# Router to first expert product in fewer steps: masks, ranks and first hits shortened, residual products ahead of them, gather and turn in halves

## The chip, the cores and the metric

The kernel runs on one core of one Trainium2 chip. The metric is the device time of one execution in microseconds (us), as the median over several executions.

## What is computed

Two layers (DEPTH = 2) over 256 tokens of width 1024, all in float32. Each layer adds to the residual stream x first a mixer (three kinds of heads, not touched here), then a mixture of experts. The latter, cut to what matters:

```python
gl = (xf @ w_group) + b_group                 # 4 groups; xf = rmsnorm(x, norm2_g)
pg = softmax(gl); g_sel = argmax(gl)
el = (xf @ w_expert) + b_expert               # 4 groups x 8 experts
top_v, top_i = lax.top_k(el[g_sel], 2)        # the best two of the group's eight
wts = softmax(top_v) * pg[g_sel]
eid = g_sel * 8 + top_i
# each of the 32 experts, on the tokens sent to it:
h = silu(xb @ w_gate[e]) * (xb @ w_up[e])     # 1024 -> 512
out = sum over the token's two experts of wts * (h @ w_down[e])
x = x + out
```

Each expert has three matrices of 2 MB, so a layer reads 96 of them.

## The kernel before

The tokens lie in two tiles of 128 partitions (NT = 2, index j), xres holds the residual stream token by token. Each engine has its own instruction list, written out by hand in the order in which it runs; semaphores (s_...) order them against each other. `V.drain()` on VectorE waits until the engine's earlier operations have landed, so that the next may read them.

**Expert stage.** Experts go in 16 pairs (NPAIR). One pass handles up to 32 tokens (UT) of each expert of a pair: 64 slots. A pair takes as many passes as its fuller expert needs, which is known on the chip only; the counts go to `ctl`, and the engines read their loop bounds from there. A pass (`one_pass` on each engine) does the gate product (L1462, kind 0, from `xTe`), adds the last pass's result to the sums in PSUM banks 4 to 7 (`combine`, L1434), does the up product (L1462, kind 1), gathers the rows of the next pass (`gather`, L1415: `hit` times xres), turns hx and the weighted hits (L1475, L1479), turns the gathered rows (L1424, weights `rows_g[r, k::KD]`) and does the down product (L1499). ScalarE copies the gathered rows from PSUM (L602), VectorE builds the next hits (L851, L854), the SwiGLU (L874 to L881) and `xTe` (L843, a multiply by the norm's gain).

**The ring.** Weights pass through ten tiles of 2 MB, loaded by SyncE's queue in the order of use. A tile's next load waits for the product that used it (`tile_free`). The first ten matrices of a layer are loaded during the mixer as its buffers come free; the last two of them wait for the mixer's output product.

**Router to first expert product**, the stretch that the change rewrites. TensorE turns xres (L1402), runs one product that nobody reads (`busy(1)`, L1810), then the router product (L1818, 36 columns: 4 groups, 32 experts) into bank 0. Four more such products follow, then TensorE waits for the masks (s_mk). VectorE reads the logits (L1279), takes maxima and their indices for the group and then for the experts of the group (L1286 to L1304), and makes the masks `mk` and their sum `mks` (L1314, L1316). TensorE then computes for each token how many earlier ones went to each expert, and each expert's count, all in bank 1 (L1825 to L1829), puts xres into banks 4 to 7 by a product with the identity (L1832), and waits for the hits of the first pair (s_hit0). VectorE makes these from the ranks of experts 0 and 1 (L1330 to L1337, then L851, L854), then the slot of every token, the number of passes per pair and the control values (L1340 to L1379, s_ctl), reads two of these back into registers (L1381, L1382) and only then waits for the turned rows and makes `xTe` (s_xte0). SyncE and GpSimd wait for s_ctl too, before they load the next layer's small parameters. ScalarE computes two exponentials of the router (L805, L807) between.

## Time and profile before

| | |
|---|---|
| median of 3 executions | 1297.69 us (1297.36 to 1298.72) |
| the profiled execution | 1291.37 us |
| its span, from the first instruction to the last | 1289.6 us |
| TensorE busy | 1070.8 us (83%) |
| VectorE, ScalarE, GpSimd busy | 460.6, 179.9, 23.7 us |
| DMA | 440.56 MB, mean 342 GB/s |
| chain that ended last | PE 52%, DMA 41%, DVE 3%, issue 2% |

The tables of the profile are read so. PE is TensorE, PEld its weight loads, DVE VectorE, ACT ScalarE, POOL GpSimd, SPq the queue of SyncE. A line like L1462 is a line of the kernel. A float32 product shows as two matmul records. "issue" is time in which an engine waited for nothing that the profile shows, its own register work among it; DVEq is the engine's sequencer. The granted clock (PEclk) is the share of TensorE's full clock of 2.4 GHz, so 0.50 is 1.2 GHz. Durations of one engine's operations overlap a little, so the chain's pieces, not the durations, add up.

### The profile page before, as it was taken

The page shows a single profiled execution, that of the slowest core. Times are in us where ns is not written, and L with a number is a line of the kernel's source. Part 1 is how long each engine was busy: PE and PEld are TensorE (multiplying, and loading weights), DVE is VectorE, ACT ScalarE, POOL GpSimd, SP SyncE. Part 2 cuts the span into 40 slices and gives each one's busy share as a digit, 9 for nine tenths or more (in the row PEclk, how much of TensorE's full clock was granted, in tenths as well). Part 3 has the DMA queues.
Part 4 walks back from the last instruction along what each step waited for, and adds up shares of the span by engine and source line. Part 5 has one row for each costly group of instructions (what it writes and reads, how often), then busy time and mean ns, then how long its engine had stood idle before and what let it go on. Part 6 is the DMA issues. An engine that isn't in the chain of part 4 may idle for free.

```text
span 1289.6 us, 23165 instructions
## 1 busy us (share of the span) xinstructions
PE 1070.8 (83%) x9476; PEld 576.8 (45%) x9477; DVE 460.6 (36%) x1253; ACT 179.9 (14%) x427; POOL 23.7 (2%) x36
## 2 busy tenths in 40 slices
PE   5999999997887766776799999898767777679966
PEld 3476654453333333333355755543333333334433
DVE  0786445433232222222237753533222222224321
ACT  2224310010010000000024160100000000001000
POOL 3000002000000000000000000000000000000000
PEclk8999999998998888888899999998888888889988
DMA  9621378999999999999993313799999999996997
GB/s 313 228 104 66 137 296 288 383 427 426 426 427 427 426 427 426 426 427 427 387 332 140 131 66 131 326 376 427 426 424 427 428 426 428 425 426 277 428 428 297
DMA packets 50270, 440.56 MB, mean 342 GB/s; under 512 B 9313, under 2 KB 11521, under 8 KB 25089
## 3 DMA queue, kind: packets, MB, share of 16 engines
q1 hardware_dynamic: 48112, 435.79, 81.7%
q0 software_dynamic: 960, 1.51, 0.7%
q10 hardware_dynamic: 1104, 1.85, 0.5%
q8 instruction: 79, 1.29, 0.4%
q14 instruction: 15, 0.11, 0.0%
HBM read 437.56 MB, written 1.05 MB: 340 GB/s over the span
## 4 chain that ended last, share of the span: by engine, by line
PE 52%; DMA 41%; DVE 3%; issue 2%; DVEq 1%; ACT 0%; SPq 0%; ACTq 0%
DMA ring<-in_e_w_up_dram 24%; PE PS L1462 12%; DMA ring<-in_e_w_down_dram 9%; PE PS L1525 8%; DMA ring<-in_e_w_gate_dram 7%; PE PS L1499 6%; PE PS L1761 4%; PE PS L1519 3%; PE PS L1424 3%; PE PS L1415 3%; PE PS L1434 2%; DMA gT<-in_norm_g_dram 1%; PE PS L1695 1%; PE PS L1715 1%; PE PS L1475 1%
## 5 line engine op out<-in xcount | busy, mean ns | idle before, releaser
L1462 PE MATMUL PS<-ring,hT 128*32 128x256 f32 x4608 | 336.5, 452 | 171.6 <-DMA ring<-in_e_w_gate_dram 112.4
L1462 PEld LDWEIGHTS PS<-ring,hT 128*32 128x32 f32 x4608 | 182.6, 125 | 347.0 <-issue 283.4
L1499 PE MATMUL PS<-ring,hT 128*32 128x512 f32 x1152 | 137.1, 618 | 11.5 <-DMA ring<-in_e_w_down_dram 11.5
L874 DVE TENSOR_SCALAR hT<-hT 128x256 f32<-128x256 f32 x36 | 10.6, 294 | 334.1 <-ACT hT L607 334.1
L1525 PE MATMUL PS<-ring,hT 128*128 128x512 f32 x256 | 113.1, 595 | 0.0
L1424 PE MATMUL PS<-cst,mixT 64*64 64x64 f32 x1216 | 81.2, 282 | 5.8 <-ACT mixT L602 1.4
L1424 PEld LDWEIGHTS PS<-cst,mixT 64*64 64x64 f32 x1216 | 77.1, 212 | 15.0 <-issue 11.8
L1415 PE MATMUL PS<-xres,scr 128*64 128x512 f32 x304 | 73.6, 605 | 0.0
L1499 PEld LDWEIGHTS PS<-ring,hT 128*32 128x32 f32 x1152 | 36.4, 113 | 82.7 <-issue 80.8
L1434 PE MATMUL PS<-hT 64*128 64x512 f32 x288 | 71.8, 615 | 0.0
L1525 PEld LDWEIGHTS PS<-ring,hT 128*128 128x128 f32 x256 | 47.5, 190 | 53.6 <-issue 53.6
L881 DVE TENSOR_TENSOR hT<-hT,PS 128x256 f32<-128x256 f32 x36 | 15.2, 421 | 156.5 <-PE PS L1462 156.5
L602 ACT COPY mixT<-PS 128x512 f32<-128x512 f32 x38 | 22.2, 585 | 335.7 <-PE PS L1415 335.7
L876 DVE RECIPROCAL hT<-hT 128x256 f32<-128x256 f32 x36 | 63.1, 1753 | 2.6
L1761 PE MATMUL PS<-ring,mixT 128*128 128x512 f32 x128 | 57.8, 599 | 2.1 <-DVE mixT L1262 1.9
L607 ACT ACTIVATE hT<-PS 128x256 f32<-128x256 f32 x36 | 13.8, 383 | 292.8 <-PE PS L1462 292.8
L612 ACT COPY hT<-PS 128x512 f32<-128x512 f32 x36 | 21.1, 585 | 221.4 <-PE PS L1499 221.4
L843 DVE TENSOR_TENSOR hT<-PS,gT 128x512 f32<-128x512 f32 x38 | 26.3, 692 | 70.2 <-PE PS L1424 70.2
L1519 PE MATMUL PS<-hT,ring 128*128 128x256 f32 x192 | 45.6, 399 | 2.6 <-ACT hT L625 2.6
L1519 PEld LDWEIGHTS PS<-hT,ring 128*128 128x128 f32 x192 | 38.2, 201 | 9.1 <-issue 3.7
L883 DVE COPY hT<-PS 128x256 f32<-128x256 f32 x36 | 15.3, 425 | 74.8 <-PE PS L1479 74.8
L1434 PEld LDWEIGHTS PS<-hT 64*128 64x128 f32 x288 | 25.5, 186 | 32.1 <-issue 32.1
(342 smaller groups left out, 898.4 us busy)
## 6 DMA issues: line engine op xcount, KB each, us to landing
ring<-in_e_w_gate_dram SPq DMA_DIRECT2D x64, 2048.0 KB, 38.6
ring<-in_e_w_up_dram SPq DMA_DIRECT2D x64, 2048.0 KB, 39.8
ring<-in_e_w_down_dram SPq DMA_DIRECT2D x60, 2048.0 KB, 37.3
ring<-in_w_in_dram SPq DMA_DIRECT2D x10, 2048.0 KB, 18.5
ring<-in_w_out_dram SPq DMA_DIRECT2D x2, 4096.0 KB, 13.0
ring<-in_e_w_down_dram SPq DMA_DIRECT2D x8, 1024.0 KB, 38.7
ring<-in_w_in_dram SPq DMA_DIRECT2D x2, 1024.0 KB, 23.2
xres<-in_x_dram ACTq DMA_DIRECT2D x1, 1024.0 KB, 9.9
```

The source lines that it names most:

```text
L602: act.copy(rows_g, PS[:, 0, :]).then_inc(gs, 1)
L612: act.copy(Y, PS[:, 3, :]).then_inc(s_ys, 1)
L843: V.tensor_tensor(xTe, PS[:, 0, :].rearrange("p (k s) -> p k s", k=KD), bcast(gT[:, l, 1, :], PAIR), ALU.mult).then_inc(xte, 1)
L876: V.reciprocal(es, es)
L1415: last = pe.matmul(PS[64 * h:64 * h + 64, 0, :], hit[:, j, :], xres[:, j, 512 * h:512 * h + 512], start=j == 0, stop=j == NT - 1)
L1424: last = pe.matmul(PS[r, 0, PAIR * k:PAIR * k + PAIR], rows_g[r, k::KD], ident[r, r], start=True, stop=True)
L1434: pe.matmul(PS[:, 4 + 2 * j + h, :], hitT[r, j, :], Y[r, :], start=False, stop=False)
L1462: last = pe.matmul(PS[o:o + UT, bank, 0:256], xTe[:, k, UT * u:UT * u + UT], w[u][:, k, :, 2 * h:2 * h + 2], start=k == 0, stop=k == KD - 1)
L1499: last = pe.matmul(PS[o:o + UT, 3, :], hTe[:, c % 2, hc:hc + UT], w[u][:, c, 512 * h:512 * h + 512], start=c == 0, stop=c == KF - 1)
L1519: last = pe.matmul(PS[:, bank, T * half:T * half + T], wchunk(c)[:, k, col:col + P], hT[:, k, :], start=k == 0, stop=k == KD - 1)
L1525: last = pe.matmul(PS[:, bank, :], hT[:, k, P * j:P * j + P], wchunk(c)[:, k, 0:512], start=k == 0, stop=k == KD - 1)
L1761: last = pe.matmul(PS[:, OUT_BANK[n], :], mixT[:, k, P * j:P * j + P], wout[:, k, 512 * h:512 * h + 512], start=k == 2, stop=k == 1)
```

## The change

All of it lies between the router product and the middle of the first expert product of each layer.

- TensorE: the product without a reader ahead of the router product goes, and the four behind it. In their place, ahead of the wait for the masks, come the products that put xres into banks 4 to 7. The ranks of both token tiles come from two products over 64 columns (`mks` has a block of zeros ahead for that) and raise s_rk by themselves; the counts come from two products into bank 2 with a semaphore of their own (s_cn); then one product without a reader, and the wait for the hits.
- VectorE: the group logits go straight into `gl8`, the expert logits into `lg`; memsets move ahead. The sum and reciprocal of the group exponentials, and the weights `wgt`, move behind the first pair's rows. The first hits come from one operation over the ranks and the summed masks, and four compares of 32 columns straight into `hit`. Then passes per pair and control values (s_ctl), then `xTe` in two halves, then the slots of all tokens and the weights, and then the two register reads.
- The first gather is done in halves of 256 columns into banks 0 and 3, with the columns of xres read in the order k, p (a step of 8 words), so that `rows_g` holds each k contiguously. ScalarE copies each half, TensorE turns each half, VectorE multiplies each half; s_gath0, s_gs0, s_rT0 and s_xte0 count twice per layer. The first expert product waits for the first half at its start, and for the second ahead of k = 4.

```diff
@@ -805,7 +803,9 @@
                 act.activation(pex, pex, ACT.Exp).then_inc(s_rge, 1)
                 act.wait_ge(s_rv, l + 1)
                 act.activation(dif, dif, ACT.Exp).then_inc(s_rve, 1)
-                rows_gathered(s_gath0, s_gs0, l)
+                for c in range(2):
+                    act.wait_ge(s_gath0, 2 * l + c + 1)
+                    act.copy(rows_g[:, 256 * c:256 * c + 256], PS[:, (0, 3)[c], 0:256]).then_inc(s_gs0, 1)
                 wait_apart(act, s_ctl, l + 1)
                 total = act.value_load(c_tot, min_val=NPAIR, max_val=MAXN - 1)
                 p0 = act.value_load(c_p0, min_val=0, max_val=(L - 1) * (MAXN - 1))
...
@@ -1272,30 +1269,33 @@
                 norm_rows(l, 1)
 
 
+                V.memset(gl8, -3.0e38)
+                V.memset(mks[:, 0, :], 0.0)
+                V.drain()
                 parameters(dve, 2, l)
                 dve.wait_ge(s_rp, l + 1)
                 dve.wait_ge(s_rs, 2 * l + 2)
                 for j in range(NT):
-                    V.scalar_tensor_tensor(lg[:, j, :], PS[:, 0, 64 * j:64 * j + 36], rs[:, j:j + 1], rb[:, :], ALU.mult,
-                                           ALU.add)
-                V.memset(gl8, -3.0e38)
-                V.drain()
-                V.tensor_copy(gl8[:, :, 0:4], lg[:, :, 0:4])
+                    V.scalar_tensor_tensor(gl8[:, j, 0:4], PS[:, 0, 64 * j:64 * j + 4], rs[:, j:j + 1], rb[:, 0:4],
+                                           ALU.mult, ALU.add)
+                for j in range(NT):
+                    V.scalar_tensor_tensor(lg[:, j, :], PS[:, 0, 64 * j + 4:64 * j + 36], rs[:, j:j + 1], rb[:, 4:36],
+                                           ALU.mult, ALU.add)
                 V.drain()
                 for j in range(NT):
                     V.max(gmx[:, j, :], gl8[:, j, :])
                 V.drain()
                 for j in range(NT):
                     V.max_index(idx[:, 0, j, :], gmx[:, j, :], gl8[:, j, :])
-                V.tensor_tensor(pex, lg[:, :, 0:4], gmx[:, :, 0:1].broadcast_to([P, NT, 4]), ALU.subtract).then_inc(s_rg, 1)
                 V.drain()
                 V.tensor_copy(gsel, idx[:, 0, :, 0:1])
                 V.drain()
 
                 gid = cst[:, C_GID:C_GID + NE].unsqueeze(1).broadcast_to([P, NT, NE])
                 V.tensor_tensor(elp, gid, gsel.broadcast_to([P, NT, NE]), ALU.not_equal)
-                V.drain()
-                V.scalar_tensor_tensor(elp, elp, NEG, lg[:, :, 4:36], ALU.mult, ALU.add)
+                V.tensor_tensor(pex, gl8[:, :, 0:4], gmx[:, :, 0:1].broadcast_to([P, NT, 4]), ALU.subtract).then_inc(s_rg, 1)
+                V.drain()
+                V.scalar_tensor_tensor(elp, elp, NEG, lg, ALU.mult, ALU.add)
                 V.drain()
                 for j in range(NT):
                     V.max(emx[:, j, :], elp[:, j, :])
@@ -1305,82 +1305,83 @@
                 V.tensor_tensor(dif, emx[:, :, 1:2], emx[:, :, 0:1], ALU.subtract).then_inc(s_rv, 1)
                 V.drain()
                 V.tensor_copy(eid, idx[:, 1, :, 0:2])
-                dve.wait_ge(s_rge, l + 1)
-                V.tensor_reduce(pgs, pex, X, ALU.add)
-                V.drain()
-                V.reciprocal(pgs, pgs)
+                V.drain()
                 iota_e = cst[:, C_T:C_T + NE].unsqueeze(1).broadcast_to([P, NT, NE])
                 for a in range(2):
                     V.tensor_tensor(mk[:, a], iota_e, eid[:, :, a:a + 1].broadcast_to([P, NT, NE]), ALU.is_equal)
                 V.drain()
-                V.tensor_tensor(mks, mk[:, 0], mk[:, 1], ALU.add).then_inc(s_mk, 1)
+                V.tensor_tensor(mks[:, 1:], mk[:, 0], mk[:, 1], ALU.add).then_inc(s_mk, 1)
+                V.memset(Y, 0.0)
+                V.memset(hitT, 0.0)
+                V.drain()
+
+
+                ranks = PS[:, 1, 0:64].rearrange("p (j n) -> p j n", j=NT)
+                dve.wait_ge(s_rk, l + 1)
+                V.scalar_tensor_tensor(fsh, ranks[:, :, 0:2], 1.0, mks[:, 1:, 0:2], ALU.add, ALU.mult)
+                V.drain()
+                for j in range(NT):
+                    for u in range(2):
+                        last = V.tensor_scalar(hit[:, j, UT * u:UT * u + UT], cst[:, C_T + 1:C_T + 1 + UT], fsh[:, j, u:u + 1],
+                                               rs[:, j:j + 1], ALU.is_equal, ALU.mult)
+                last.then_inc(s_hit0, 1)
+
+
+                dve.wait_ge(s_cn, l + 1)
+                nf = nu.rearrange("p i u -> p (i u)")
+                V.tensor_scalar(nf, PS[:, 2, 0:NE], 1.0, 1.0 / UT, ALU.max, ALU.mult)
+                V.tensor_copy(rnk, ranks)
+                V.drain()
+                V.tensor_scalar(nf, nf, 31.0 / 64, ROUND, ALU.add, ALU.add)
+                V.tensor_scalar(fr32, rnk, 1.0 / UT, -31.0 / 64, ALU.mult, ALU.add)
+                V.drain()
+                V.tensor_scalar(nf, nf, -ROUND, None, ALU.add)
+                V.drain()
+                V.tensor_tensor(npass, nu[:, :, 0], nu[:, :, 1], ALU.max)
+                V.drain()
+                V.tensor_tensor_scan(pend, cst[:, C_ONES:C_ONES + NPAIR], npass, 0.0, ALU.mult, ALU.add)
+                V.tensor_copy(ctl[:, C_NP:C_NP + NPAIR], npass[0:1, :])
+                V.tensor_copy(c_p0, past[:, 0:1])
+                V.drain()
+                V.tensor_scalar(upr, pend[0:1, :], past[:, 0:1], None, ALU.add)
+                V.tensor_copy(c_tot, pend[0:1, NPAIR - 1:NPAIR])
+                V.drain()
+                V.tensor_copy(ctl[:, C_PASS + 1:C_PASS + 1 + NPAIR], upr).then_inc(s_ctl, 1)
+                V.tensor_copy(past[:, 0:1], upr[:, NPAIR - 1:NPAIR])
+                for c in range(2):
+                    dve.wait_ge(s_rT0, 2 * l + c + 1)
+                    V.tensor_tensor(xTe[:, 4 * c:4 * c + 4, :], PS[:, (0, 3)[c], 0:256].rearrange("p (k s) -> p k s", k=4),
+                                    bcast(gT[:, l, 1, 4 * c:4 * c + 4], PAIR), ALU.mult).then_inc(s_xte0, 1)
+
+                V.tensor_scalar(fr32, fr32, ROUND, -ROUND, ALU.add, ALU.add)
+                V.tensor_tensor(pst[:, :, 0], pend, npass, ALU.subtract)
+                V.drain()
+                V.scalar_tensor_tensor(rnk, fr32, float(UT), rnk, ALU.mult, ALU.add)
+                V.tensor_scalar(pst[:, :, 1], pst[:, :, 0], float(PAIR), float(UT), ALU.mult, ALU.add)
+                V.tensor_scalar(pst[:, :, 0], pst[:, :, 0], float(PAIR), None, ALU.mult)
+                V.drain()
+                V.tensor_tensor(rnk, rnk, rv[:, 160:192].unsqueeze(1).broadcast_to([P, NT, NE]), ALU.add)
+                dve.wait_ge(s_rge, l + 1)
+                V.tensor_reduce(pgs, pex, X, ALU.add)
+                V.drain()
+                for a in range(2):
+                    V.tensor_tensor(rtm[:, a], mk[:, a], rnk, ALU.mult)
+                V.reciprocal(pgs, pgs)
                 dve.wait_ge(s_rve, l + 1)
                 V.tensor_scalar(wgt[:, :, 0:1], dif, 1.0, None, ALU.add)
                 V.drain()
+                V.tensor_reduce(sh.rearrange("p a j -> p (a j)"), rtm.rearrange("p a j n -> p (a j) n"), X, ALU.add)
                 V.reciprocal(wgt[:, :, 0:1], wgt[:, :, 0:1])
                 V.drain()
+                V.tensor_copy(sw, sh)
                 V.tensor_tensor(wgt[:, :, 0:1], wgt[:, :, 0:1], pgs, ALU.mult)
                 V.drain()
+                V.tensor_scalar(sh, sh, -float(PAIR), None, ALU.add)
                 V.tensor_tensor(wgt[:, :, 1:2], wgt[:, :, 0:1], dif, ALU.mult)
-                V.memset(Y, 0.0)
-                V.memset(hitT, 0.0)
-
-                dve.wait_ge(s_rk, l + 1)
-                ranks = PS[:, 1, 0:64].rearrange("p (j n) -> p j n", j=NT)[:, :, 0:2]
-                V.tensor_tensor(fpl, ranks, cst[:, C_T + 1:C_TT:UT].unsqueeze(1).broadcast_to([P, NT, 2]), ALU.add)
-                for a in range(2):
-                    V.scalar_tensor_tensor(fmk[:, a], ranks, UT - 0.5, mk[:, a, :, 0:2], ALU.is_lt, ALU.mult)
-                V.drain()
-                for a in range(2):
-                    V.tensor_tensor(fmk[:, a], fmk[:, a], fpl, ALU.mult)
-                V.drain()
-                V.tensor_reduce(fsh.rearrange("p a j -> p (a j)"), fmk.rearrange("p a j u -> p (a j) u"), X, ALU.add)
-                V.drain()
-                row_hits(s_hit0, cst[:, C_T + 1:C_TT], fsh)
-                V.tensor_copy(rnk, PS[:, 1, 0:64].rearrange("p (j n) -> p j n", j=NT))
-                V.tensor_copy(cnt, PS[:, 1, 64:96])
-                V.drain()
-                nf = nu.rearrange("p i u -> p (i u)")
-                V.tensor_scalar(nf, cnt, 1.0, 1.0 / UT, ALU.max, ALU.mult)
-                V.tensor_scalar(fr32, rnk, 1.0 / UT, -31.0 / 64, ALU.mult, ALU.add)
-                V.drain()
-                V.tensor_scalar(nf, nf, 31.0 / 64, ROUND, ALU.add, ALU.add)
-                V.drain()
-                V.tensor_scalar(nf, nf, -ROUND, None, ALU.add)
-                V.drain()
-                V.tensor_tensor(npass, nu[:, :, 0], nu[:, :, 1], ALU.max)
-                V.tensor_scalar(fr32, fr32, ROUND, -ROUND, ALU.add, ALU.add)
-                V.drain()
-                V.tensor_tensor_scan(pend, cst[:, C_ONES:C_ONES + NPAIR], npass, 0.0, ALU.mult, ALU.add)
-                V.scalar_tensor_tensor(rnk, fr32, float(UT), rnk, ALU.mult, ALU.add)
-                V.drain()
-                V.tensor_tensor(pst[:, :, 0], pend, npass, ALU.subtract)
-                V.drain()
-                V.tensor_scalar(pst[:, :, 1], pst[:, :, 0], float(PAIR), float(UT), ALU.mult, ALU.add)
-                V.tensor_scalar(pst[:, :, 0], pst[:, :, 0], float(PAIR), None, ALU.mult)
-                V.drain()
-                V.tensor_tensor(rnk, rnk, rv[:, 160:192].unsqueeze(1).broadcast_to([P, NT, NE]), ALU.add)
-                V.drain()
-                for a in range(2):
-                    V.tensor_tensor(rtm[:, a], mk[:, a], rnk, ALU.mult)
-                V.drain()
-                V.tensor_reduce(sh.rearrange("p a j -> p (a j)"), rtm.rearrange("p a j n -> p (a j) n"), X, ALU.add)
-                V.drain()
-                V.tensor_copy(sw, sh)
-                V.drain()
-                V.tensor_scalar(sh, sh, -float(PAIR), None, ALU.add)
-
-                V.tensor_scalar(upr, pend[0:1, :], past[:, 0:1], None, ALU.add)
-                V.tensor_copy(c_p0, past[:, 0:1])
-                V.tensor_copy(c_tot, pend[0:1, NPAIR - 1:NPAIR])
-                V.tensor_copy(ctl[:, C_NP:C_NP + NPAIR], npass[0:1, :])
-                V.drain()
-                V.tensor_copy(past[:, 0:1], upr[:, NPAIR - 1:NPAIR])
-                V.tensor_copy(ctl[:, C_PASS + 1:C_PASS + 1 + NPAIR], upr).then_inc(s_ctl, 1)
+                V.drain()
                 wait_apart(dve, s_ctl, l + 1)
                 total = dve.value_load(c_tot, min_val=NPAIR, max_val=MAXN - 1)
                 p0 = dve.value_load(c_p0, min_val=0, max_val=(L - 1) * (MAXN - 1))
-                rows_turned(l, s_rT0, s_xte0, l)
                 with dve.Fori(0, total) as q:
                     one_pass(l, p0 + q)
@@ -1456,6 +1457,8 @@
 
                     w = [t.rearrange("p (k n c) -> p k n c", k=KD, c=KF) for t in weights(kind)]
                     for k in range(KD):
+                        if kind == 0 and k == KD // 2:
+                            pe.wait_ge(s_xte0, 2 * l + 2)
                         for h in range(2):
                             for u in range(2):
                                 o = 64 * h + UT * u
@@ -1463,7 +1466,7 @@
                                                  w[u][:, k, :, 2 * h:2 * h + 2], start=k == 0, stop=k == KD - 1)
                     last.then_inc(s_used[kind], 1)
 
-                pe.wait_ge(s_xte0, l + 1)
+                pe.wait_ge(s_xte0, 2 * l + 1)
                 pe.wait_ge(s_xte, n + 1)
                 in_product(0, 1)
                 combine(n)
@@ -1807,10 +1810,9 @@
                 def busy(n):
 
                     for k in range(n):
-                        pe.matmul(PS[:, 4 + 2 * (k % 2), :], ident, cst[:, 0:512], start=True, stop=True)
+                        pe.matmul(PS[:, 3, :], ident, cst[:, 0:512], start=True, stop=True)
 
                 turn_xs(l, 1)
-                busy(1)
                 parameters(pe, 2, l)
                 for j in range(NT):
                     turned_xs(l, 1, j)
@@ -1819,21 +1821,34 @@
                                          start=k == 0, stop=k == KD - 1)
                 last.then_inc(s_rp, 1)
 
-                busy(4)
-                pe.wait_ge(s_mk, l + 1)
-                bef = cst[:, C_BEFORE:C_BEFORE + P]
-                pe.matmul(PS[:, 1, 0:NE], bef, mks[:, 0, :], start=True, stop=True)
-                pe.matmul(PS[:, 1, NE:2 * NE], ones, mks[:, 0, :], start=True, stop=False)
-                pe.matmul(PS[:, 1, NE:2 * NE], bef, mks[:, 1, :], start=False, stop=True)
-                pe.matmul(PS[:, 1, 2 * NE:3 * NE], ones, mks[:, 0, :], start=True, stop=False)
-                pe.matmul(PS[:, 1, 2 * NE:3 * NE], ones, mks[:, 1, :], start=False, stop=True).then_inc(s_rk, 1)
                 for j in range(NT):
                     for h in range(2):
                         pe.matmul(PS[:, 4 + 2 * j + h, :], ident, xres[:, j, 512 * h:512 * h + 512], start=True, stop=False)
+                pe.wait_ge(s_mk, l + 1)
+                flat_mks = mks.rearrange("p j n -> p (j n)")
+                bef = cst[:, C_BEFORE:C_BEFORE + P]
+                pe.matmul(PS[:, 1, 0:2 * NE], bef, flat_mks[:, NE:3 * NE], start=True, stop=False)
+                pe.matmul(PS[:, 1, 0:2 * NE], ones, flat_mks[:, 0:2 * NE], start=False, stop=True).then_inc(s_rk, 1)
+                pe.matmul(PS[:, 2, 0:NE], ones, mks[:, 1, :], start=True, stop=False)
+                pe.matmul(PS[:, 2, 0:NE], ones, mks[:, 2, :], start=False, stop=True).then_inc(s_cn, 1)
+                busy(1)
+
                 pe.wait_ge(s_hit0, l + 1)
-                gather(s_gath0)
-                pe.wait_ge(s_gs0, l + 1)
-                turn_gathered(s_rT0)
+                for c in range(2):
+                    for j in range(NT):
+                        for h in range(2):
+                            half = xres[:, j, 512 * h:512 * h + 512].rearrange("t (p k) -> t k p", k=KD)
+                            last = pe.matmul(PS[64 * h:64 * h + 64, (0, 3)[c], 0:256], hit[:, j, :], half[:, 4 * c:4 * c + 4, :],
+                                             start=j == 0, stop=j == NT - 1)
+                    last.then_inc(s_gath0, 1)
+                for c in range(2):
+                    pe.wait_ge(s_gs0, 2 * l + c + 1)
+                    for k in range(4 * c, 4 * c + 4):
+                        for h in range(2):
+                            r = slice(64 * h, 64 * h + 64)
+                            last = pe.matmul(PS[r, (0, 3)[c], PAIR * (k % 4):PAIR * (k % 4) + PAIR],
+                                             rows_g[r, 64 * k:64 * k + 64], ident[r, r], start=True, stop=True)
+                    last.then_inc(s_rT0, 1)
 
                 wait_apart(pe, s_ctl, l + 1)
 
```

## Rows read from the trace of the kernel before

**Rows 1.** Windows: us, busy per engine (instructions), granted clock, DMA share, GB/s

```profile
198.60:200.60 2.00, 1.93 (x9) 0.47 (x8) 1.63 (x12) 0.03 (x1) 0.00 (x0) 1.00 0.67 287
...
831.00:833.20 2.20, 2.14 (x32) 2.00 (x32) 1.09 (x9) 0.00 (x0) 0.00 (x0) 1.00 0.38 160
...
834.80:838.20 3.40, 3.40 (x33) 1.93 (x37) 2.26 (x11) 0.00 (x0) 0.00 (x0) 0.50 0.00 0
...
193.40:198.60 5.20, 5.20 (x12) 2.14 (x11) 4.29 (x27) 0.00 (x0) 0.00 (x0) 0.70 1.02 438
...
240.00:250.00 10.00, 10.00 (x144) 4.95 (x138) 3.04 (x6) 0.97 (x2) 0.00 (x0) 1.00 0.72 277
...
380.00:640.00 260.00, 181.94 (x1846) 90.69 (x1840) 57.42 (x160) 15.59 (x34) 0.00 (x0) 0.86 1.01 426
```

**Rows 2.** Chain of waits, layer 0: start us, us, what

```profile
180.95 1.94 PE PS L1402 x16
182.89 0.86 PE PS L1810 x2
183.75 3.51 PE PS L1818 x32
...
191.87 0.24 DVE so L1316
...
192.15 0.41 PE PS L1825 x2
...
193.23 0.42 PE PS L1829 x2
193.66 5.00 PE PS L1832 x8
198.66 1.89 PE PS L1415 x8
...
200.57 0.59 ACT mixT L602
...
201.21 2.16 PE PS L1424 x32
...
204.55 3.83 PE PS L1462 x64
```

**Rows 3.** Timeline, both layers: start us, us, engine, line, operation, tiles

```profile
181.88 2.25 ACT L625 ACTIVATE hT<-PS,gT 128x128 f32<-128x128 f32 x8 [2.45 <-PE PS L1402]
...
208.66 0.93 SPq L507 DMA_DIRECT2D ring<-in_e_w_down_dram  x2
...
824.79 3.68 PE L1832 MATMUL PS<-xres,cst 128*128 128x512 f32 x8
...
834.79 5.43 PE L1462 MATMUL PS<-ring,hT 128*32 128x256 f32 x64 [1.63 <-DVE hT L843]
```

**Rows 4.** Chain of waits, layer 1

```profile
815.58 3.51 PE PS L1818 x32
...
823.37 0.23 DVE so L1316
...
832.36 0.32 DVEq L1381
...
833.64 0.70 DVE hT L843
```

**Rows 5.** Groups by line and shape, 187 to 206: count, busy us, mean ns, idle before

```profile
L851 DVE TENSOR_SCALAR scr<-cst,so,small 128x64 f32<-128x64 f32 x5 | 1.3, 312 | 0.1
...
L1325 DVE MEMSET hT<- 128x512 f32 x1 | 0.5, 485 | 0.1
...
L1344 DVE TENSOR_SCALAR vm<-vm 128x32 f32<-128x32 f32 x1 | 0.2, 181 | 0.1
```

**Rows 6.** The page's groups over both layers

```profile
L876 DVE RECIPROCAL hT<-hT 128x256 f32<-128x256 f32 x36 | 63.1, 1753 | 2.6
L607 ACT ACTIVATE hT<-PS 128x256 f32<-128x256 f32 x36 | 13.8, 383 | 292.8 <-PE PS L1462 292.8
```

26 lines of the change are left out of this document (11 added, 15 removed).

## Prediction

> **What bounds the kernel now.** I read the windows first. From 250 us to the last product of layer 0 the DMA engines are full: the row 380:640 has DMA share 1.01 at 426 GB/s while PE works 182 of 260 us. The expert stage is a stream of 2 MB matrices, and nothing that shortens PE inside it counts. What does count is when the stream is released. The ten ring tiles are filled ahead; the fill ends in row 198.6:200.6 (share 0.67 of 2.0 us, so at 199.9) and in row 831:833.2 (0.38 of 2.2, so at 831.8), and row 834.8:838.2 has the DMA at nothing [rows 1]. It waits for the first expert product to give tiles back: SP issues the next pair of matrices at 208.66, right behind that product (204.55 to 208.38) [rows 2, 3]. So the start of the first product sets the start of the stream, in each of the two layers. The stretch before 250, with the DMA at 277 GB/s in 240:250 [rows 1], hangs on PE, which started with the same product. A microsecond taken out between the mixer and the first product should arrive at the end of the kernel as a microsecond, twice.
>
> Then I read the chain of waits through that stretch. Layer 0 [rows 2]: router product until 187.26 (183.75 + 3.51), masks ready at 192.11 (191.87 + 0.24), rank and count products until 193.66, the residual products until 198.66, gather 1.89, copy 0.59, turn until 203.37, first product at 204.55. So 17.29 us from the router product's end. The chain goes over PE: the hits wait finished while PE works off the residual products. These took 5.00 us at a granted clock of 0.70 in that stretch (1.2 GHz part of the time) [rows 1]; in layer 1 the same took 3.68 [rows 3]. Layer 1 [rows 4]: router product until 819.09, masks at 823.60 (823.37 + 0.23), first product at 834.79, 15.70 us. There the chain goes through DVE, whose list of rank and control steps and two value loads (832.36 to 833.64) holds back the last multiply; and the first product itself took 5.43 us at clock 0.50 [rows 1, 3], against 3.83 in layer 0 [rows 2].
>
> **The change, step by step, per layer.**
> (a) Router product. The cover product ahead of it goes (0.86 in the chain [rows 2]). What is next to be late is ACT's half of hT: 8 operations from 181.88 in 2.25 us [rows 3], so the first four end at about 183.0 (estimate, half the time); a weight load behind that gives a start at about 183.3 instead of 183.75. I take 0.4 of a possible 0.86.
> (b) Router product to masks. Before, 4.51 us in layer 1 and 4.85 in layer 0 [rows 2, 4]; layer 0's surplus has no operation to it. A copy and a memset leave the path ahead of the first maximum, two more operations from PSUM enter: I take 0.1 gained. The sum and the reciprocal of the group's exponentials leave the stretch between the expert index and the masks; one dependent step is about 0.26 (0.18 for a small operation [rows 5] and 0.08 of drain): 0.2 gained. So 4.2 in layer 1; in layer 0, 4.5.
> (c) Masks to gather. PE: residual products already done: 3.68 us from the router product's end, against 4.2 to 4.5 for the masks, so they are off the path by 0.5 us (at the low clock, 5.0, they would be late by that much). Then 4 small products instead of 5: of the 5 the first took 0.41, the middle three 0.22 each ((193.23 - 192.15 - 0.41)/3), the last 0.42 [rows 2]. Four are 0.05 + 0.41 + 2x0.22 + 0.42 = 1.3; ranks alone, two of them, are ready at 0.9. Then one cover product, 0.92 (a quarter of 3.68 [rows 3]): PE is free for the gather 2.3 after the masks. DVE: the two memsets (0.49 and about half of that for the smaller one [rows 5]) plus drain are done at 0.8, so DVE waits for the ranks until 0.9; one operation and drain 0.25; four of 128x32. Of 128x64 four take 4x0.31 at most; at 32 wide a similar one is 0.18 [rows 5]: 0.7. Hits at 1.85. The new wait is for PE's cover product, not for the hits: gather at 2.3. Before it was 6.55 in layer 0 and 4.9 in layer 1 (824.79 + 3.68) [rows 2, 3].
> (d) Gather. Same columns in two halves: 1.9 [rows 2]. The moving operand now steps 8 words (32 bytes). No row has that as moving operand. Nearest below: the turn of xres reads its stationary operand with that step, 16 in 1.94 = 0.121 us each, against 0.110 (3.51/32) for contiguous ones in the router product [rows 2], at most 10% more. Nearest in the number of streams: the expert product reads four streams with two words in every 16 bytes at 3.83 for 64 [rows 2], which is as many different 16-byte stretches per time as two streams of single words. I take no price; bounds 0 and 1.9.
> (e) Copies and turns. The copy of half 0 (0.38 for 128x256, 0.59 for 128x512 [rows 2, 6]) runs under the gather of half 1, that of half 1 under the turn of half 0 (half of 2.16). So gather and turn stand back to back: 1.9 + 2.15. The turn now reads contiguous rows; I take nothing for it (at most 0.2).
> (f) Turn to first product. Only half 0 of xTe is needed: its multiply (0.70 at 512 wide [rows 4], so some 0.4) runs under the turn of half 1. What is left is PE's own register work (two value loads, tile waits). Before, product minus end of turn was 1.18 in layer 0 with 0.70 of DVE in it: between 0.45 and 1.18 remains, since the cover of that multiply is gone. I take 0.8, nearer the middle. The product's wait for half 1 at its middle comes 1.9 us in, when that multiply is long done.
> (g) SP and GpSimd wait for the control values, which come about 4 us after the masks (1.85 to the hits and some eight dependent steps of 0.26), where in layer 1 they now come 8.8 after them (832.36 [rows 4]). In layer 0 their small parameter loads then start under the end of the ring's fill. The last two matrices of the fill are for the second pair, which PE reaches more than 11 us after the first product's start (rival 2); cost nothing, and 6 us of delay would still be hidden.
>
> Sum from masks: 2.3 + 1.9 + 2.15 + 0.8 = 7.15. Layer 0: 187.26 - 0.4 + 4.5 + 7.15 = 198.5 against 204.55: 6.0. Layer 1: 819.09 - 0.4 + 4.2 + 7.15 = 830.0 against 834.79: 4.8. Together 10.8. Clock: layer 1 gets back 5.43 - 3.83 = 1.6 if its first product runs at full clock; the stretches of idle PE are shorter than before (1.2 and 1.6 ahead of the product), but not gone. I reckon with one low spell left among the two layers, -1.5. Net **10.9 us**.
>
> The page's execution took 1291.37 us with a span of 1289.6: by the sum 1280.5 and 1278.7. The median shown is 1297.69, 6.3 above the profiled execution; I lay the same difference on it: **1286.8 us**. The cap: the stream can't be released before the ring's fill ends. It ends at 199.9 and 831.8, release is now expected at 198.5 + 3.9 = 202.4 and 830.0 + 3.9 = 833.9. Two microseconds remain in each layer, so the gain passes, though at most 2 more per layer would.
>
> **Rivals.**
> 1. The strided gather streams at half rate. For it: two streams, each word in its own 16 bytes, and no row with it. Against it: the rows in (d). Price 1.9 per layer: 1286.8 + 3.8 = 1290.6. Beside it: the Trainium skill (Advanced Engine Details and Errata, SBUF Cachelines) says that at least two hits on a 16-byte line are needed to absorb the access latency and that a different line per access costs. It gives no figure; by that rule rival 1 or rival 4 would hold, and the stationary read at 0.121 against 0.110 bears it out only by a tenth [rows 2].
> 2. DVE is late in the first pass. What was taken off the path (slot numbers, weights: some 10 dependent steps of 0.26 to 0.45, then 1.28 for value loads [rows 4]) runs after the second multiply, to about 10.9 after the masks; two rounds of hits follow (3 us, from 0.31 an operation [rows 5]), to 13.9, which is 6.8 after the product's start; then the SwiGLU steps, about 3.4 with the reciprocal's 1.75 in them [rows 6], end at 10.2. PE asks for them at 3.8 + 1.9 + 3.8 + 1.9 = 11.4. Slack 1.2. If the list is 2.5 us longer than I count, 1.3 per layer are lost: 1289.4.
> 3. The gain is absorbed: the stream's end is set by something else than the first product (fill and parameters in one queue, the cap above). Then 1297.7. Against it: the DMA idle from 199.9 to 208.66 and at 834.8 [rows 1, 3].
> 4. Slower: the strided read costs much more than twice. One mechanism, the moving operand of the gather, 1.9 us a layer at rate 1. The gain of 10.9 is eaten at 1 + 10.9/3.8 = 3.9 times the time; at 5 times it is 1297.69 - 10.9 + 15.2 = 1302.0. Against it: stationary reads with this step.
>
> **How the numbers follow.** Forecast 0.69 (its own range 1283 to 1289.5: (a) and (f) at their good ends and no low spell give 3 to 4 less; two low spells and (f) at 1.18 give 2.3 more), rival 1 0.12, rival 2 0.06, rival 3 0.08, rival 4 0.05. Faster by over 0.2% (about what a measurement of this kernel can tell from no change, here 2.6 us) is the first three: 0.87; same 0.08; slower 0.05. The range takes the forecast's own and rival 1: 1283 to 1291.5.
>
> **What would show it.** In the profile after: residual products right behind the router product and done before the first rank product; masks about 4.2 behind the router product; gather of both halves 1.9 (3.8: rival 1; 9: rival 4); the first expert product 11.3 to 11.7 behind the router product's end, at 198.5 and, less what layer 0 gave, 11.3 behind in layer 1; the DMA idle ahead of it down from 8 to some 2 us; the stretch from first product to the layer's end as long as before (rival 3: longer by the gain; rival 2: an idle PE ahead of the transpose of hx in the first pass). Wrong would be: the first product late for registers or for code by several us, or more low-clock spells than one.

## The result and the profile after

The changed kernel takes 1290.45 us (median of 13 executions, 1286.10 to 1295.13) against 1297.36 us (13 executions, 1294.04 to 1301.60) of the kernel before: ratio 0.9946, 95% interval 0.9930 to 0.9963. So 6.9 us were gained, where 10.9 had been forecast; the forecast of 1286.8 us was 3.7 too low. The result lies inside the stated range of 1283 to 1291.5, but outside the forecast's own part of it (1283 to 1289.5), in the part that rival 1 had added. The profiled execution took 1290.15 us, with a span of 1288.3.

The chain of waits of the changed kernel in layer 0 (start us, us, what), the counterpart of [rows 2]:

```profile
182.82 0.90 PE PS L1403 x8
...
183.75 1.15 ACT hT L623 x4
...
185.03 3.73 PE PS L1820 x32
188.77 5.21 PE PS L1826 x8
193.97 0.17 PE PS L1830 x2
...
194.79 0.94 PE PS L1813 x2
195.73 3.81 PE PS L1841 x16
199.53 1.18 PE PS L1849 x32
...
200.74 0.44 DVE hT L1353
201.17 1.40 issue
202.58 5.34 PE PS L1465 x61
207.92 1.92 PE PS L1435 x8
```

L1820 is the router product, L1826 the residual products (xres into banks 4 to 7), L1830 the first rank product, L1813 the cover product (one that nobody reads), L1841 the gather, L1849 the turn, L1465 the expert product, L1435 the combine behind it. The whole stretch now runs over TensorE, but for ScalarE's four activations and one multiply of VectorE (L1353); VectorE's long list of dependent steps, which held the chain of layer 1 before [rows 4], is gone from it. Layer 1 repeats it:

```profile
814.24 0.90 PE PS L1403 x8
...
820.19 5.21 PE PS L1826 x8
825.39 0.17 PE PS L1830 x2
...
827.14 3.81 PE PS L1841 x16
830.95 1.18 PE PS L1849 x32
...
832.59 1.18 issue
833.78 5.42 PE PS L1465 x60
839.19 1.92 PE PS L1435 x8
```

**A clock for the stretch.** The mixer ahead runs identical code, yet ends at different times. So I count from the end of the mixer's last product, which is where the turn of xres starts in the chain (180.95 and 812.78 before, 182.82 and 814.24 after), and give two numbers per layer: "to start", until the first expert product starts, and "to end", until it ends (the start of the combine), since the ring's tiles are given back there. Before: 23.60 and 27.43 in layer 0, 22.01 and 27.44 in layer 1. After: 19.76 and 25.10, 19.54 and 24.95. To the start 3.8 and 2.5 were gained, to the end 2.3 and 2.5. Behind that, nothing changed in this pair of executions: from the first product's end to the start of the layer's last combine it is 439.5 us before (208.38 to 647.91) and 439.3 after (207.92 to 647.19), and in layer 1 442.8 (840.22 to 1283.03) and 442.6 (839.19 to 1281.80).

In windows of the changed kernel (columns as in [rows 1]) the clock is low in two places of this stretch, in both layers, the residual products and the first expert product; the kernel before had one such place in each layer of its first profiled execution:

```profile
188.70:194.00 5.30, 5.30 (x12) 2.29 (x11) 4.20 (x27) 0.41 (x2) 0.00 (x0) 0.68 1.00 419
...
202.60:206.00 3.40, 3.40 (x36) 1.83 (x40) 1.45 (x11) 0.00 (x0) 3.40 (x6) 0.54 0.89 127
...
820.20:825.40 5.20, 5.20 (x11) 2.18 (x10) 4.26 (x27) 0.41 (x2) 0.00 (x0) 0.68 1.02 435
...
833.80:837.20 3.40, 3.40 (x33) 1.78 (x37) 1.50 (x11) 0.00 (x0) 0.00 (x0) 0.50 0.02 7
```

### The profile page after: what moved, and what is told of

Its sections match the earlier page's. It is cut to its first block, busy times and chain, and to the rows that moved or that the text cites. A ratio compares the mean times of both kernels' runs of the same rounds, so it can differ in the third digit from the quotient of the medians.

```text
span 1288.3 us, 23141 instructions
## 1 busy us (share of the span) xinstructions
PE 1072.1 (83%) x9472; PEld 575.7 (45%) x9473; DVE 458.6 (36%) x1245; ACT 180.3 (14%) x429; POOL 23.8 (2%) x36
## 3 DMA queue, kind: packets, MB, share of 16 engines
q10 hardware_dynamic: 1104, 1.85, 0.5%
## 4 chain that ended last, share of the span: by engine, by line
PE 56%; DMA 41%; issue 1%; ACT 1%; SPq 0%; ACTq 0%; DVE 0%; DVEq 0%
DMA ring<-in_e_w_up_dram 30%; PE PS L1465 12%; PE PS L1528 9%; PE PS L1502 6%; DMA ring<-in_e_w_down_dram 6%; PE PS L1764 5%; PE PS L1425 3%; PE PS L1522 3%; DMA ring<-in_e_w_gate_dram 3%; PE PS L1416 3%; PE PS L1435 2%; PE PS L1698 1%; DMA gT<-in_norm_g_dram 1%; PE PS L1826 1%; PE PS L1718 1%
## 5 line engine op out<-in xcount | busy, mean ns | idle before, releaser
L1465 PE MATMUL PS<-ring,hT 128*32 128x256 f32 x4608 | 338.7, 454 | 172.9 <-DMA ring<-in_e_w_gate_dram 117.2
L1465 PEld LDWEIGHTS PS<-ring,hT 128*32 128x32 f32 x4608 | 182.6, 126 | 350.4 <-issue 286.8
L1502 PE MATMUL PS<-ring,hT 128*32 128x512 f32 x1152 | 134.3, 607 | 12.6 <-DMA ring<-in_e_w_down_dram 12.6
L1528 PE MATMUL PS<-ring,hT 128*128 128x512 f32 x256 | 116.5, 609 | 0.0
L1425 PE MATMUL PS<-cst,mixT 64*64 64x64 f32 x1152 | 76.9, 282 | 4.4
L1425 PEld LDWEIGHTS PS<-cst,mixT 64*64 64x64 f32 x1152 | 73.0, 212 | 11.9 <-issue 11.9
L1435 PE MATMUL PS<-hT 64*128 64x512 f32 x288 | 71.8, 615 | 0.0
L1416 PE MATMUL PS<-xres,scr 128*64 128x512 f32 x288 | 69.7, 605 | 0.0
L1764 PE MATMUL PS<-ring,mixT 128*128 128x512 f32 x128 | 60.8, 625 | 2.1 <-DVE mixT L1259 1.9
L1435 PEld LDWEIGHTS PS<-hT 64*128 64x128 f32 x288 | 25.5, 186 | 32.2 <-issue 32.2
```

Source lines behind the costliest of these rows:

```text
L1416: last = pe.matmul(PS[64 * h:64 * h + 64, 0, :], hit[:, j, :], xres[:, j, 512 * h:512 * h + 512], start=j == 0, stop=j == NT - 1)
L1425: last = pe.matmul(PS[r, 0, PAIR * k:PAIR * k + PAIR], rows_g[r, k::KD], ident[r, r], start=True, stop=True)
L1435: pe.matmul(PS[:, 4 + 2 * j + h, :], hitT[r, j, :], Y[r, :], start=False, stop=False)
L1465: last = pe.matmul(PS[o:o + UT, bank, 0:256], xTe[:, k, UT * u:UT * u + UT], w[u][:, k, :, 2 * h:2 * h + 2], start=k == 0, stop=k == KD - 1)
L1502: last = pe.matmul(PS[o:o + UT, 3, :], hTe[:, c % 2, hc:hc + UT], w[u][:, c, 512 * h:512 * h + 512], start=c == 0, stop=c == KF - 1)
L1528: last = pe.matmul(PS[:, bank, :], hT[:, k, P * j:P * j + P], wchunk(c)[:, k, 0:512], start=k == 0, stop=k == KD - 1)
```

## Experiments

All numbers of a stretch are from one profiled execution each; "to start" and "to end" are counted as above, from the mixer's last product. Ratios are to the kernel before, timed beside the run. Where no median is given, the profiled execution is the only one.

**Is it the step in the gather, or the halves?** The gather took 3.81 us where 1.9 was forecast. Two things had changed in it: the step of 8 words and the splitting. The first kernel keeps the step and gathers in one piece (ScalarE still copies in two):

```diff
...
-                for c in range(2):
-                    for j in range(NT):
-                        for h in range(2):
-                            half = xres[:, j, 512 * h:512 * h + 512].rearrange("t (p k) -> t k p", k=KD)
-                            last = pe.matmul(PS[64 * h:64 * h + 64, (0, 3)[c], 0:256], hit[:, j, :], half[:, 4 * c:4 * c + 4, :], ...)
+                for j in range(NT):
+                    for h in range(2):
+                        half = xres[:, j, 512 * h:512 * h + 512].rearrange("t (p k) -> t k p", k=KD)
+                        last = pe.matmul(PS[64 * h:64 * h + 64, 0, :], hit[:, j, :], half, start=j == 0, stop=j == NT - 1)
...
```

> Changed kernel, but the first gather is one piece again: two token tiles by two halves, 512 columns each, still read with a step of 8 words. Theory (the step costs): the gather takes 3.8 us as in two halves, because the rate of the strided read is halved. Rival (the splitting costs: shorter products, two banks): the gather takes 1.9 us as in the kernel before. Turn stays at 1.2 us, since its rows stay contiguous.

It took 1286.73 us, with a mixer that ended at 180.93. From its chain, the gather in both layers:

```profile
193.99 3.89 PE PS L1840 x8
...
198.60 1.17 PE PS L1847 x32
...
824.90 3.82 PE PS L1840 x8
```

Eight records of 512 columns, 3.89 and 3.82 us. The step halves the rate of the moving operand (1.89 without it [rows 2]), and the splitting costs nothing. The turn stays at 1.17.

**Gather, copy, turn and multiply as before, the rest of the change kept:**

```diff
...
+                rows_turned(l, s_rT0, s_xte0, l)
...
+                gather(s_gath0)
+                pe.wait_ge(s_gs0, l + 1)
+                turn_gathered(s_rT0)
...
```

> Changed kernel with gather, copy, turn and multiply as in the kernel before (contiguous read, one piece, turn with a step of 8 words); the rest of the change stays. Theory (step in the gather costs 1.9, contiguous turn gives back 1.0, register work of 1.9 us behind the last issued turn is a floor): gather 1.9, copy 0.6, turn 2.15, product 1.2 behind the turn, so 5.9 from the gather's start to the product against 6.86 and 6.64 in the changed kernel: about 0.8 us a layer faster than the changed kernel, ratio to the kernel before about 0.993. Rival (the halves pay as planned): slower than the changed kernel by 1 us or more a layer.

Median 1288.0 us, ratio 0.9928 (0.9900 to 0.9956).

```profile
195.86 1.89 PE PS L1411 x8
...
197.77 0.59 ACT mixT L600
...
198.41 2.16 PE PS L1420 x32
...
200.59 0.70 DVE hT L841
201.29 0.45 issue
201.74 3.87 PE PS L1458 x62
```

From the gather's start to the product 5.88 and 5.89 us, against 6.85 (195.73 to 202.58) and 6.64 in the changed kernel. To start 18.78 and 18.79, to end 22.66 and 22.63. So gather and turn in halves, as built, cost 1.0 and 0.75 us in the two layers instead of paying, and the whole gain comes from the other parts of the change. The timed medians go the same way, 1288.0 against 1290.45, though their intervals overlap. In this execution the first product ran at full clock besides (3.87 and 3.85 us).

**What is the wait behind the turn?** "issue" of 1.40 and 1.18 us stands behind the multiply of the second half, 1.87 and 1.65 behind the turn's end. Two products that nobody reads are put there:

```diff
                 wait_apart(pe, s_ctl, l + 1)
+                for k in range(2):
+                    pe.matmul(PS[:, 2, :], ident, cst[:, 0:512], start=True, stop=True)
```

> Changed kernel with two products without a reader (1.84 us at full clock, into bank 2) behind the turn and the wait for the control values, ahead of the value loads. Theory (behind the turn TensorE's array is idle for 1.9 us only because its sequencer loads registers): the sequencer loads them while the two products run, the first expert product starts within 0.2 us of where it did, 1.9 behind the turn, and if the idle stretch is what lets the clock fall, that product takes 3.8 us instead of 5.4, 1.5 a layer. Rival 1 (the wait is for something else, VectorE or the ring): the product starts 1.0 to 1.8 us later. Rival 2 (the clock falls for the narrow products before, not for the idle stretch): the product keeps its 5.4 us.

```profile
201.94 1.16 PE PS L1849 x32
203.10 1.91 PE PS L1855 x4
205.02 3.85 PE PS L1465 x63
```

1.91 us of products went in, and the expert product starts 1.92 behind the turn, where it started 1.87 behind it (layer 1: 1.91 against 1.65): to start 19.79 both, against 19.76 and 19.54. So the array isn't needed in this wait, and two products fit under it for nothing in layer 0 and for 0.25 us in layer 1. By itself the run doesn't tell the sequencer's own work (waits, two value loads, loop bounds, tile waits) from an event outside, which would hide the products as well; the rival's "1.0 to 1.8 us later" doesn't follow from it. The run with early value loads, further down, decides for the sequencer. The first expert product took 3.85 and 3.80 us, so it was at full clock; to end 23.64 and 23.59, 1.4 better. The timing doesn't show it: 1290.99 us, ratio 0.9958 (0.9940 to 0.9977), the same as the changed kernel within the intervals. The trace says where it went: behind the first product, to the layer's last combine, this execution needs 440.7 us (208.87 to 649.55) and 443.9 (840.21 to 1284.13), where the changed kernel has 439.3 and 442.6. That is 1.4 and 1.3 longer, all of what the full clock gave. Why the rest gets longer is not shown. And low spells lay in the mixer, which ended at 185.23, 2.4 later than in the changed kernel's first execution.

**The step where it costs nothing.** The gather is contiguous and whole; ScalarE's two copies read PSUM with the step and write k by k, and turn and multiply keep their halves (now in banks 3 and 0):

```diff
...
+                src = PS[:, 0, :].rearrange("s (p k) -> s k p", k=KD)
                 for c in range(2):
-                    act.copy(rows_g[:, 256 * c:256 * c + 256], PS[:, (0, 3)[c], 0:256]).then_inc(s_gs0, 1)
+                    act.copy(rows_g[:, 256 * c:256 * c + 256].rearrange("s (k p) -> s k p", k=4),
+                             src[:, 4 * c:4 * c + 4, :]).then_inc(s_gs0, 1)
...
```

> Changed kernel with a contiguous gather in one piece into bank 0; ScalarE's two copies read it with the step of 8 words and write k by k, turn and multiply stay in halves with contiguous rows. Theory (the step costs only where TensorE streams it): gather 1.9, first copy 0.4, turn 1.2 to 1.6 (second copy under the first half's turn), product 1.7 to 1.9 behind: 5.3 to 5.7 against 6.86 and 6.64, so 1.1 to 1.4 us a layer faster than the changed kernel. Rival (the step costs ScalarE the same way): copies of 0.8 each, turn ended 0.8 later, nothing left of the gain.

Median 1287.03 us, ratio 0.9917 (0.9890 to 0.9944).

```profile
196.03 1.89 PE PS L1418 x8
...
197.95 0.38 ACT mixT L809
...
198.37 1.17 PE PS L1845 x32
...
199.57 0.44 DVE hT L1355
200.00 1.28 issue
201.29 3.86 PE PS L1467 x60
```

The copy with the step takes 0.38 us, like one without (0.37 in the changed kernel). Gather to product 5.26 and 5.00 us; to start 18.17 and 17.91, to end 22.03 and 21.79: 3 us per layer better than the changed kernel, 1.6 of it from these parts and 1.5 from a first product at full clock. Not all of that arrives: behind the first product layer 0 needs 440.9 us here (205.15 to 646.02), 1.6 more than in the changed kernel, layer 1 the same 442.6.

**The residual products ahead of the masks**, undone: they go back behind the count products, in the place of the cover product, with `busy(4)` ahead of the wait for the masks.

```diff
-                for j in range(NT):
-                    for h in range(2):
-                        pe.matmul(PS[:, 4 + 2 * j + h, :], ident, xres[:, j, 512 * h:512 * h + 512], start=True, stop=False)
+                busy(4)
                 pe.wait_ge(s_mk, l + 1)
...
-                busy(1)
+                for j in range(NT):
+                    for h in range(2):
+                        pe.matmul(PS[:, 4 + 2 * j + h, :], ident, xres[:, j, 512 * h:512 * h + 512], start=True, stop=False)
```

> Changed kernel with the residual products back behind the rank and count products (in the place of the one cover product), and four cover products ahead of the wait for the masks, as in the kernel before. Theory of the prediction (that move takes the residual products off the path, 3.68 us less the one cover product of 0.92): the gather starts about 5.0 us behind the masks at full clock instead of 2.4, the first product 2.6 us later per layer. Rival (VectorE's hits would have come then anyway): under 1 us later.

It took 1293.22 us. Masks at 192.71, gather at 197.67: 4.96 behind them, where the changed kernel has 2.38 (193.35 to 195.73). To start 22.31 and 22.11 (182.21 to 204.52, 816.69 to 838.80) against 19.76 and 19.54: 2.56 later, as forecast. Undoing this move alone costs 2.6 us per layer, and what is left of the change then gains next to nothing: the kernel before has 22.65 and 22.0 in its later executions (below). The reverse, the move alone in the kernel before, was not run. By the trace it would gain nothing in layer 1: there the turn is done by 833.2 [rows 1], and VectorE's own list only at 833.64 [rows 4]. So the move needs the shorter list of VectorE beside it.

**The cover products.** One put back ahead of the router product:

```diff
                 turn_xs(l, 1)
+                pe.matmul(PS[:, 4, :], ident, cst[:, 0:512], start=True, stop=True)
```

> Changed kernel with the one product without a reader put back ahead of the router product. Theory (the idle and narrow stretch around the router product is what drops the clock in the residual products): these take 3.7 us instead of 5.2, the rank products start with the masks and the gather 0.3 us earlier against the masks, while the router product starts 0.3 us later; first product unchanged within 0.3. Rival (the clock falls for another reason): residual products stay at 5.2 us and all is 0.3 later.

It took 1290.98 us. The residual products stayed at 5.18 and 5.06 us: my reason for that low spell fell. To start 20.11 and 19.84, 0.3 later, as the rival has it. The first product, though, took 3.87 and 3.86. And the one ahead of the gather taken out:

```diff
-                busy(1)
```

> Changed kernel without the one cover product between the count products and the gather. Theory of the prediction (TensorE, not VectorE's hits, sets the gather's start, by the cover product): the gather starts up to 0.3 us earlier against the masks, not more, because the hits come then. Rival: the clock falls in the gather and it takes over 4.5 us instead of 3.8.

It took 1289.66 us.

```profile
194.51 0.42 DVE scr L1325 x2
194.94 0.04 issue
194.98 3.88 PE PS L1840 x15
```

Now the chain runs over VectorE's hits (L1325). The gather starts 2.27 and 2.46 behind the masks instead of 2.38 and 2.56; to start 19.70 and 19.51. The cover product cost 0.1 us. The hits come 0.1 ahead of its end, not 0.45 as step (c) has it.

**Value loads under the gather.** On the kernel with the reordering copies, the first pair is taken out of TensorE's loop, and its registers are read between gather and turn:

```diff
...
+                pe.wait_ge(s_ctl, l + 1)
+                passes0 = pe.value_load(ctl[0:1, C_NP:C_NP + 1], min_val=1, max_val=MAXN // 2)
+                past0 = pe.value_load(ctl[0:1, C_PASS:C_PASS + 1], min_val=0, max_val=L * MAXN)
                 for c in range(2):
                     pe.wait_ge(s_gs0, 2 * l + c + 1)
...
+                with pe.Fori(0, passes0) as q:
+                    one_pass(l, past0 + q, 0, 0)
+                with pe.Fori(0, 2) as i5:
+                    for i in range(1, 6):
...
```

> The kernel with the contiguous gather and the reordering copies, and the first pair taken out of TensorE's loop: its two value loads stand between the gather and the turn, where they run under the gather. Theory (1.7 to 1.9 us of register work behind the last issued turn is the floor of the first product, and most of it is the wait and the two value loads): the product starts 0.6 to 1.2 us behind the turn instead of 1.7, so 0.5 to 1.1 us a layer earlier. Rival 1 (the tile waits and the code of the pass are the floor): no gain. Rival 2 (eleven bodies of the pair in place of six cost code loading): the expert stage gets longer by several us.

Median 1285.18 us, ratio 0.9891 (0.9862 to 0.9919), the fastest of all; its interval overlaps that of the kernel it builds on.

```profile
198.57 1.89 PE PS L1418 x8
...
201.14 0.90 issue
202.04 0.70 PE PS L1848 x16
...
202.77 0.44 DVE hT L1355
203.20 0.24 issue
203.44 3.85 PE PS L1467 x64
```

The product starts 0.70 and 0.69 behind the turn instead of 1.75 and 1.49, so most of that wait was TensorE's own loads; but 0.90 and 0.68 us of them now stand ahead of the turn. Net, from the gather's start to the product 4.87 and 4.64 against 5.26 and 5.00: 0.4 us per layer. The expert stage is not several us longer for the eleven bodies of the pair: behind the first product 441.5 and 442.6 us, against 440.9 and 442.6 in the kernel that it builds on.

**Does the profiled execution of before stand for the others?** It took 1291.37 us, 6 less than the median, and by the profiled executions alone the change would have gained 1.2 us. Both kernels were profiled again, unchanged.

> The kernel before, unchanged, profiled a second time. Its first profiled execution took 1291.4 us against a median of 1297.4, and in it TensorE's clock fell on none of the mixer's products. Theory (that execution was a fast one: the low spells fall elsewhere from execution to execution, and most cost 1.5 us in the mixer or the router): here the mixer of layer 0 ends 1.5 to 4 us later than 180.95, and the stretch from there to the end of the first expert product stays at 27.4 us or above. Rival (the mixer of the changed kernel is slower than that of the kernel before): the mixer ends at 181 again.

> The same once more: theory and rival as in the run before; of interest is how far the stretch from the mixer's last product to the end of the first expert product spreads over executions of one kernel (theory: 27.4 to 30.5 us, a low spell more or less).

> The changed kernel, unchanged, profiled a second time. Theory: gather 3.8, turn 1.2 and product 1.65 to 1.9 behind the turn again in both layers; the stretch from the mixer's last product to the end of the first expert product 25.0 us, or 23.5 where no spell of the low clock meets that product.

They took 1293.29, 1295.24 and 1292.49 us. The kernel before, second time, layer 0:

```profile
204.44 0.70 DVE hT L843
205.14 0.45 issue
205.59 5.43 PE PS L1462 x64
211.02 1.92 PE PS L1434 x8
```

| | clock granted, 60 to 180 us | mixer's last product ends | to start | to end |
|---|---|---|---|---|
| before, first | 1.00 | 180.95, 812.78 | 23.60, 22.01 | 27.43, 27.44 |
| before, second | 0.97 | 182.94, 815.07 | 22.65, 22.02 | 28.08, 27.45 |
| before, third | 0.94 | 184.87, 816.98 | 22.64, 22.01 | 28.07, 27.45 |
| after, first | 0.97 | 182.82, 814.24 | 19.76, 19.54 | 25.10, 24.95 |
| after, second | 0.94 | 185.19, 813.84 | 19.71, 21.21 | 23.56, 25.07 |

The mixer of the kernel before ended 2.0 and 3.9 us later in layer 0 than in the first execution. So the changed kernel's mixer is not slower. What sets its end is how much of it met a low clock. Over all thirteen profiled executions, of either kernel and of the runs, a mean clock of 1.00 from 60 to 180 us goes with an end at 180.9 (two), 0.97 with 182.2 to 183.7 (seven), 0.94 with 184.9 to 185.7 (four). In its second and third execution the chain of the kernel before ran over VectorE in both layers; in layer 0 the low spell lay in the four cover products of L1810 (4.95 us for them) and not in the residual products, where it costs, so to start it has 22.65 in place of 23.60.

The stretch "to end" has a mean of 27.65 before and 24.67 after: 3.0 us per layer, 6.0 in the kernel, against 6.9 timed (4.8 to 9.1 by the interval). The second execution of after has a new case in layer 1: router product 4.31 and residual products 6.30 us. The rank products waited 1.9 us for the residual products, and the gather started 3.66 behind the masks in place of 2.56: the cover of step (c) can fail by 1.1 us. The run with early value loads has the same in layer 1 (4.36 and 6.25). Behind the first product that layer of the second execution took 445.2 us, where all three executions of before have 442.4 to 442.8.

## Why the prediction was right in part

The mechanism held: the stretch between mixer and first product sets the release of the stream, both layers gain, and what is gained arrives in the pair of executions compared (439.5 against 439.3 us behind it in layer 0, 442.8 against 442.6 in layer 1). Rival 3 is out, and so is rival 2: in the changed kernel the first pass runs from its up product (209.84) to its gather (213.59) to the turn (216.24) with the same distances as before (210.30, 214.06 and 216.71 there, within 0.01), with no idle TensorE. Rival 4 is out. **Rival 1 is what happened**, and other terms of the sum were off beside it. That its 1290.6 us is met within 0.2 is luck in part: the turn gave back 1.0 per layer that nobody had counted, and (b), (c) and (f) took 2.5 over both layers. Of the signs named, the idle DMA ahead of the release came out at 6 us in layer 1, not 2 (by the shares from 831.5 us on the fill ends at 833.2, and SP issues next at 839.47): the ring's fill ends 19.0 us behind the mixer, before and after, and the product came later than forecast. Step (g) held: the control values came 4.3 behind the masks (197.63), and the small parameter loads went out from 197.66 on.

- (a) Router product 0.4 earlier: from the mixer's last product to the router product's end it was 6.31, now 5.94 (182.82 to 188.76). Right in its size, by two parts that nearly cancel: the router product starts 0.6 earlier and takes 3.73 in place of 3.51. The group of four activations that it waits for is in the chain, as named.
- (b) Router product to masks 4.2 and 4.5: measured 4.40 (masks at 824.58) and 4.59 (193.35). The sum was 0.1 to 0.2 too low. In layer 1 the way to the first maximum takes 0.85 us as before (820.18 to 821.03, 819.09 to 819.94), so the four operations from PSUM eat what the copy and the memset gave, and the step taken out gave 0.1.
- (c) Masks to gather 2.3: 2.38 and 2.56. Nearly right, and the residual move is worth 2.6. But the hits were to be ready at 1.85 and came at 2.27 in the run without the cover product: the rank products ended later, and the four compares took 0.9 in place of 0.7. Not foreseen: the residual products run into the low clock, 5.21 us in place of 3.68, and end 0.6 and 0.8 behind the masks. That costs little, because the rank products then start without their first delay (0.17 for the first in the chain instead of 0.41).
- (d) **Gather 1.9: measured 3.81.** This is the step that failed. "I take no price" rested on two rows, and neither was of that kind. The stationary read with the step (0.121 against 0.110 us [rows 2]) is another operand. The four streams of the expert product have two words in every 16 bytes, and I argued that two streams of single words ask for as many 16-byte stretches. By the run with the whole gather the moving operand with one word in every 32 bytes takes twice the time. The Trainium skill's rule that was put beside rival 1 (Advanced Engine Details and Errata, SBUF Cachelines) wants at least two hits on a line. The traces agree: the factor is 2.0 for this operand and this step.
- (e) Gather and turn back to back, turn 2.15: back to back was right, but the turn took 1.18. I had allowed 0.2 for its rows being contiguous. In the stationary operand 32 records of 64 columns take 2.16 with the step and 1.17 without. By the same rule of the Trainium skill the step costs there too, and the traces agree. So the order change gave back 1.0 of the 1.9 that it cost.
- (f) Turn to product 0.8, bounded by 1.18: measured 1.87 and 1.65, outside the bound. The bound was read as product start minus the end of the turn. It should have been counted from the turn's start, as it seems: from there the product came 3.34 us later before (201.21 to 204.55), and 3.05 and 2.83 later now, though the turn itself is 1.0 shorter. My reading is that the sequencer runs ahead of the array in the long turn and does part of its register work (1.9 us in layer 0, 1.65 in layer 1) under it, and that the turn of 1.18 us leaves it no such lead; this is worked out from the traces, no run changes the turn's length by itself. What is shown is that the work is the sequencer's: two cover products fit under it, and with the value loads moved the product starts 0.7 behind the turn. So what the turn gave back (1.0) was lost again against the sum (1.07 and 0.85 over the 0.8), and the overlap of the second half's multiply gained nothing.
- Clock: 0.1 was put in for both layers (1.6 back in layer 1, less 1.5 for one spell). In the pair of executions compared it took 1.5 instead: the two first products need 3.83 and 5.43 us before, 5.34 and 5.42 after. In the two executions of the changed kernel the first product was low in two of four layers, in the three of the kernel before in five of six, so over all of them the clock gave 1.1. These are few executions, and what a product at full clock gave was lost behind it in the run with two cover products.

To the start of the product the sum was 6.0 + 4.8 = 10.8; measured in the same pair of executions 3.84 + 2.47 = 6.3. The 4.5 missing are (d), (e) and (f) together, 6.85 and 6.64 in place of 4.85 (3.8), (b) and (c) (0.6), and rounding. The other executions of before have 22.65 in layer 0 instead of 23.60, which makes 5.4 of it. The timed 6.9, with its interval of 4.8 to 9.1, holds all of these; it can't tell them apart.

Open: why the clock falls where it does. In the windows it is granted in full until the router product's last records and at 1.2 GHz for most of the residual products in nearly all layers of the changed kernel and its variants, with a cover product ahead of the router product too. The engine is busy there, with narrow products just before. For the first expert product, low in some kernels and full in others with the same stretch ahead of it, and low in one and full in another execution of the changed kernel, no run settled the cause. So no variant's full-clock product can be put down to its edit.

## To carry to other kernels

Order a transposed or interleaved layout where the step is free, which here is ScalarE's copy out of PSUM (0.38 us with the step, 0.37 without), and keep TensorE's moving operand and stationary operand contiguous; only so did turn and multiply in halves pay (5.26 and 5.00 us from gather to product, against 5.88 with all in one piece). When a chain is shortened, ask which sequencer ran ahead under the piece that goes: by my reading of (f), register work hidden under a long piece comes out when the piece gets short. Part of it can be put under another product instead (0.4 us per layer gained of 1.1 and 0.8 moved). And read two or three executions of the kernel before ahead of a sum of a few microseconds: their mixers' ends lay 3.9 us apart, and the thirteen timings of the kernel before 7.6, with a gain of 6.9.

## What the runs showed of the hardware

- A float32 moving operand with a step of 32 bytes: 3.8 to 3.9 us for 16 records of 256 or 8 of 512 columns, against 1.89 contiguous, each for both halves of the output's partitions.
- A stationary operand with that step: 64x64 loads and products, 32 in 2.16 us against 1.17 contiguous. The turn of xres, with 128x128 loads and the same step, takes 0.121 us per record against 0.110 in the router product [rows 2], a tenth more, though the two differ in more than the step.
- TensorE's register work between the last product of a straight stretch and the first of a loop's pass (semaphore waits, two value loads, loop bounds, two tile waits): 1.87 us in layer 0 and 1.65 in layer 1; with two products of 1.91 us in all put there, 1.92 and 1.91.
- The mixer's end in layer 0 moved between 180.93 and 185.68 us over thirteen profiled executions of the same mixer code, with the mean granted clock from 60 to 180 us (1.00 to 0.94); that is more than any single part of this change.
- A first product at full clock saved 1.4 us in each layer of the run with two cover products, and 1.4 and 1.3 us were lost behind it.
